# Gate projections of six output tiles as seven block products for a pair of tiles in place of eight

## What is computed

```
z = h @ w_in                    # its last 3 x 1024 columns are the gates g
gates = sigmoid(g)
m = gates[0] * ya + gates[1] * yb + gates[2] * yc
x = layernorm(ALPHA * x + m @ w_out)
```

## Time and profile before

| | us |
|---|---|
| median of 3 runs | 2054.28 |
| the profiled execution, its own time | 2056.70 |
| its span, first to last instruction | 2054.9 |
| mix stage from the branches of tile 0 on, layer 0: 1392 matmuls | 183.51 |
| the same in layer 1 | 183.51 |

### The profile page before, as it was taken

One profiled execution on the slowest core, in us unless ns is written; L12 is line 12 of the kernel. 1 busy time (PEld: TensorE's weight loads), 2 busy tenths in 40 slices (PEclk: granted clock), 3 DMA queues, 4 the chain that ended last, 5 costly groups with the idle time before them and its releaser, 6 DMA issues.

```text
span 2054.9 us, 42901 instructions
## 1 busy us (share of the span) xinstructions
PE 2009.7 (98%) x17322; PEld 1862.5 (91%) x17322; DVE 1195.7 (58%) x2096; ACT 781.6 (38%) x1496; POOL 244.7 (12%) x262
## 2 busy tenths in 40 slices
PE   8999999999999999999999999999999999999997
PEld 8976667999999999999999766689999999999997
DVE  4864445333577652667868544453335876446676
ACT  5443345222344332334454433342222443223344
POOL 0025661000000000000002356600000000000000
PEclk9999999999999999999999999999999999999999
DMA  7349996222412222225345599942223122312261
GB/s 271 124 156 356 369 356 236 72 82 84 134 45 72 82 99 69 82 82 193 128 147 183 200 362 369 364 146 82 84 88 111 46 88 85 103 62 82 85 213 61
DMA packets 84522, 310.90 MB, mean 151 GB/s; under 512 B 10096, under 2 KB 15088, under 8 KB 84016
## 3 DMA queue, kind: packets, MB, share of 16 engines
q1 hardware_dynamic: 42480, 154.83, 23.2%
q0 software_dynamic: 37152, 144.98, 19.1%
q10 hardware_dynamic: 4768, 9.37, 1.4%
HBM read 300.84 MB, written 7.26 MB: 150 GB/s over the span
## 4 chain that ended last, share of the span: by engine, by line
PE 88%; DVE 4%; DMA 3%; ACT 2%; issue 1%; POOL 1%; DVEq 1%; PEldq 0%; ACTq 0%; PEld 0%; POOLq 0%; SPq 0%
PE PS L1021 70%; PE PS L1310 5%; PE PS L1280 5%; DMA m_RAW<-in_cache_wide,m_IDXS 2%; PE PS L1301 1%; DVE m_WL L1452 1%; PE PS L1291 1%; POOL m_RAW L497 1%; DMA m_WS<-in_w_units 1%; ACT m_WH L513 1%; PE PS L1333 1%; PE PS L1349 1%; PE PS L1340 1%; PE PS L1327 0%; ACT m_LS L536 0%
## 5 line engine op out<-in xcount | busy, mean ns | idle before, releaser
L1021 PE MATMUL PS<-m_XS,m_WH 128*128 128x288 f32 x5120 | 908.7, 295 | 10.9 <-DVE m_XS L1452 10.3
L1021 PEld LDWEIGHTS PS<-m_XS,m_WH 128*128 128x128 f32 x5120 | 759.7, 189 | 14.9 <-DVE m_WL L1452 8.1
L1021 PE MATMUL PS<-m_XS,m_WL 128*128 128x288 f32 x2560 | 580.6, 296 | 0.0
L1452 DVE TENSOR_TENSOR m_WL<-m_WS,m_WH 128x1024 fp32r<-128x1024 f32 (+1 forms) x256 | 332.6, 1301 | 200.4 <-ACT m_WH L513 186.6
L1021 PEld LDWEIGHTS PS<-m_XS,m_WL 128*128 128x128 f32 x2560 | 421.1, 188 | 0.0
L513 ACT ACTIVATE m_WH<-m_WS 128x1024 fp32r<-128x1024 f32 (+1 forms) x256 | 285.7, 1118 | 311.9 <-PE PS L1021 281.3
L497 POOL DMA_INDIRECT m_RAW<-in_cache_wide,m_IDXS x256 | 243.4, 951 | 328.0 <-PE PS L1310 99.9
L1021 PE MATMUL PS<-m_HH,m_WH 128*128 128x288 f32 x704 | 202.7, 295 | 2.2 <-DVE m_X L1517 1.9
L1021 PE MATMUL PS<-m_HL,m_WH 128*128 128x288 f32 x704 | 201.7, 295 | 0.0
L1021 PE MATMUL PS<-m_HH,m_WL 128*128 128x288 f32 x704 | 179.2, 295 | 0.0
L1021 PEld LDWEIGHTS PS<-m_HH,m_WH 128*128 128x128 f32 x704 | 132.3, 188 | 3.3 <-DVE m_WL L1452 2.3
(11 more groups left out here) (276 smaller groups left out, 2732.1 us busy)
## 6 DMA issues: line engine op xcount, KB each, us to landing
m_WS<-in_w_units SPq DMA_DIRECT2D x204, 512.0 KB
m_WS<-in_w_units SPq DMA_DIRECT2D x48, 704.0 KB
m_RAW<-in_cache_wide,m_IDXS POOLq DMA_INDIRECT x256
m_X<-in_x_t SPq DMA_DIRECT2D x6, 576.0 KB, 5.9
m_WS<-in_w_units SPq DMA_DIRECT2D x4, 576.0 KB
x_save<-m_X POOLq DMA_DIRECT2D x2, 1152.0 KB, 5.4
m_X<-x_save SPq DMA_DIRECT2D x4, 576.0 KB, 7.4
out_y<-m_X SPq DMA_DIRECT2D x8, 288.0 KB, 2.2
```

The lines of the kernel that those rows point to most:

```text
L1021: mm = pe.matmul(out(half), w(part, k), x(k)[:, half_of(half)], start=(k == 0 and part == 0 and x is xh), stop=(k == last and part == 1))
L1452: return dve.tensor_tensor(out, x, hi.bitcast(F32), ALU.subtract)
```

## The change

Tiles 0 and 1 of m stay as they are, but for work put between their steps. Tiles 2 to 7 are made as three pairs; in each pair the three gates and the branches are nine groups (three for each pair, `GROUPS = 9` in a layer). For one gate of two tiles the weights form a 2x2 block matrix (k 0-3 and 4-7 by first and second tile), and x another (k 0-3 and 4-7 by first and second 288 columns); seven products of blocks replace eight. A product is 4 steps k of one half: 12 matmuls.

- **x side, once a layer:** four VectorE operations of 128x1152 make the differences of x blocks (in place in `X`, one into `D3`), four ScalarE copies and four VectorE subtractions of 128x1152 split them (`difference_hi`, `difference_lo`). Two pairs of these stand between tiles 0 and 1, two within tile 1. As `X` is overwritten, its rows are fetched again at the end of the stage (`rows_back`: four transfers of 128x4x288).
- **weight side, per group:** two raw units land in `GATE_RAW`; VectorE makes four sums of 128x512 in place (`slot_lo`: three at product 0, one at product 4); the seven block weights are split as 128x512 slots and the two branch weights as 128x256 or 128x512 slots, nine slots a group (`PLACES`), in a ring of four. `slot_hi(s)` waits for the product of slot s-4.
- **results, per group:** products go to banks 4, 5, 6, 7, 4, 6, 7; ScalarE copies the first one to `SIG`; seven VectorE additions of 128x288 from PSUM build both gates; two sigmoids in place; then per tile the multiplication by the branch product, and from the second group of a pair on the addition into the mix; in the third group the split into `MH`, `ML`.
- Some 20 semaphores are merged into fewer with other counts, and units of `w_out` land in other raw tiles.

```diff
-                units(l, U_MIX + 2, W_MIX + 2, 30, D)
-                sp.wait_ge(S["ol_mm"], (l + 1) * 2)
+                units(l, U_MIX + 2, W_MIX + 2, 6, D)
+                sp.wait_ge(S["ol_mm"], (l + 1) * 3)
...
+                sp.wait_ge(S["gw_lo"], l * NSLOT + (GROUPS - 1) * PLACES + PRODUCTS)
+                past(sp)
+                fetch(l, U_OUT + 1, W_OUT + 1, D)
+                fetch(l, U_OUT + 3, W_OUT + 3, D)
+                sp.wait_ge(S["gp_done"], (l + 1) * GROUPS * PRODUCTS - 1)
+                past(sp)
+                rows_back(0)
+                sp.wait_ge(S["gw_lo"], (l + 1) * NSLOT)
+                past(sp)
+                fetch(l, U_OUT + 2, W_OUT + 2, D)
+                rows_back(1)
...
 # ScalarE
                 mix_tile(0, first=True)
-                with act.Fori(1, DT) as i:
-                    mix_tile(i)
+                act.wait_ge(S["t_made"], l + 1)
+                difference_hi(XR[:, first_k, early], X[:, first_k, late])
+                difference_hi(D2H[:, :, :], X[:, second_k, late])
+                mix_tile(1)
+                slot_hi(3)
+                for s in range(NSLOT):
+                    if s + 4 < NSLOT:
+                        slot_hi(s + 4)
+                    slot_after(s)
...
 # TensorE
+                def gate_product(n, r):
+                    s = n * PLACES + r
+                    if r == 4:
+                        pe.wait_ge(S["gp_copied"], l * GROUPS + n + 1)
+                    else:
+                        pe.wait_ge(S["g_sums"], (l * GROUPS + n) * 7 + max(0, r - 4))
...
+                    pe.wait_ge(S["gw_lo"], l * NSLOT + s + 1)
...
+                    for k in range(KH):
+                        mm = three(out, w(0, k), w(1, k), xh[:, k, :], xl[:, k, :], k == 0, k == KH - 1)
...
-                with pe.Fori(1, DT) as i:
-                    mix_tile(i)
+                mix_tile(1)
+                for n in range(GROUPS):
+                    for r in range(PRODUCTS):
+                        gate_product(n, r)
+                    for e in range(2):
+                        branch_product(n, e)
 # VectorE
+                def slot_lo(s):
+                    dve.wait_ge(S["gw_hi"], l * NSLOT + s + 1)
+                    lo(slot_part(1, s), slot_source(s), slot_part(0, s)).then_inc(S["gw_lo"], 1)
+                    n, r = s // PLACES, s % PLACES
+                    first, second = raw_tiles(n)
+                    if r == 0:
+                        gates_landed(dve, l, n)
+                        dve.tensor_tensor(SUM_A, in_two(second[:, lower]), in_two(second[:, upper]), ALU.add)\
+                            .then_inc(S["gw_sum"], 1)
...
+                def slot_after(s):
...
+                    if 2 <= r < PRODUCTS:
+                        slot_done(dve, l, s)
+                    if r == 2:
+                        dve.wait_ge(S["gp_copied"], l * GROUPS + n + 1)
+                        add(late_a, early_a, 6)
+                        dve.drain()
...
+                    if r >= PRODUCTS:
...
+                        dve.wait_ge(S["g_sig"], (l * GROUPS + n + 1) * 2)
+                        slot_done(dve, l, s)
+                        dve.tensor_tensor(h2(MT[:, :] if g else out), pair(e), h2(SIG[:, e, :]), ALU.mult)\
+                            .then_inc(S[f"mm_free{e}"], 1)
+                        dve.drain()
+                        if g:
+                            ins = dve.tensor_tensor(out, out, MT[:, :], ALU.add)
+                            if g == 2:
+                                ins.then_inc(S["m_sum"], 1)
+                                dve.wait_ge(S["m_hi"], l * DT + i + 1)
+                                lo(ML[:, i, :], out, MH[:, i, :]).then_inc(S["m_lo"], 1)
+                            else:
+                                dve.drain()
...
                 mix_tile(0, first=True)
-                with dve.Fori(1, DT) as i:
-                    mix_tile(i)
+                dve.tensor_tensor(D3[:, :, :], X[:, second_k, late], X[:, first_k, late], ALU.subtract)
+                dve.tensor_tensor(X[:, first_k, late], X[:, first_k, late], X[:, first_k, early], ALU.subtract)
+                dve.drain()
+                dve.tensor_tensor(X[:, second_k, late], X[:, second_k, late], X[:, first_k, late], ALU.subtract)
+                dve.drain()
+                dve.tensor_tensor(X[:, second_k, early], X[:, second_k, early], X[:, second_k, late], ALU.subtract)
+                dve.drain().then_inc(S["t_made"], 1)
+                difference_lo(1, XR[:, first_k, late], X[:, first_k, late], XR[:, first_k, early])
+                difference_lo(2, XR[:, second_k, late], X[:, second_k, late], D2H[:, :, :])
+                mix_tile(1)
+                slot_lo(3)
+                for s in range(NSLOT):
+                    slot_after(s)
+                    if s + 4 < NSLOT:
+                        slot_lo(s + 4)
+                    if s == NSLOT - 6:
+                        weight_lo(l * NU + U_OUT)
+                    if s == NSLOT - 2:
+                        weight_lo(l * NU + U_OUT + 1)
```

More of the change, by code:

```diff
@@ new lines, in branches @@
+                def branches(n):
+                    c0, width = BRANCH_AT[n % 3]
+                    for e in range(2):
+                        if n:
+                            sp.wait_ge(S["gw_lo"], l * NSLOT + (n - 1) * PLACES + PRODUCTS + e + 1)
+                            past(sp)
+                        unit = W_MIX + 4 * (2 * (FIRST_PAIR + n // 3) + e) + 3
+                        sp.dma_start(BR[e][:, 0:width], w_units[l * NW + unit, :, c0:c0 + width])\
+                            .then_inc(S[f"bw_landed{e}"], 16)
@@ new lines, in rows_back @@
+                def rows_back(half):
+                    for k in (first_k, second_k):
+                        sp.dma_start(X[:, k, half_of(half)], (x_save if l else x_t)[:, k, half_of(half)])\
+                            .then_inc(S["x_in_b" if half else "x_back"], 16)
+                gates(0)
+                for n in range(GROUPS):
+                    if n + 1 < GROUPS:
+                        gates(n + 1)
+                    else:
+                        fetch(l, U_OUT, W_OUT, D)
+                    branches(n)
@@ L453, in _ @@
+                for u in range(4, DT):
                     fetch(l, U_OUT + u, W_OUT + u, D)
@@ L913, in mix_tile @@
                     act.wait_ge(S["mm_done1"], CREDIT["mm_done1"] + l * NM + M_MIX + 3 * i + 3)
-                    weight_hi_in_loop(1, LANDING[l * NU + U_MIX + 5] + 2 * i)
+                    if first:
+                        weight_hi_in_loop(1, LANDING[l * NU + U_MIX + 5] + 2 * i)
+                    else:
+                        slot_hi(2)
                     act.wait_ge(S["m_sum"], l * DT + i + 1)
@@ L1515, in onto_rows @@
                     h = half_of(half)
+                    if back:
+                        dve.wait_ge(S["x_in_b" if half else "x_back"], 32 * (l + 1 + half))
                     dve.wait_ge(S[f"mm_done{par}"], CREDIT[f"mm_done{par}"] + l * NM + m0 + u // 2 + 1)
@@ L1986, in mix_tile @@
                         .then_inc(S["mm_free1"], 1)
-                    weight_lo_in_loop(u + 4, 0)
+                    if first:
+                        weight_lo_in_loop(u + 4, 0)
+                    else:
+                        difference_lo(3, D3L[:, :, :], D3[:, :, :], XL[:, first_k, late])
+                        difference_lo(4, XR[:, second_k, early], X[:, second_k, early], XH[:, first_k, late])
+                        slot_lo(0)
+                        slot_lo(1)
                     dve.wait_ge(S["mm_done0"], CREDIT["mm_done0"] + m + 3)
```

302 lines of the change are left out of this document (231 added, 71 removed).

## The result

The changed kernel took 2063.34 us (median of 6 runs, 2060.39 to 2066.45) against 2054.12 for the kernel before: 1.0045 times as long, 95% interval 1.0033 to 1.0057, so slower by 9 us. The forecast was 2052.3, with a range up to 2060: the time lies above that range, on the slower side. The profiled execution took 2066.45 with a span of 2064.7, against 2056.70 and 2054.9.

What follows compares the result with a forecast made beforehand. TensorE, busy 98% of the span, was taken as the bound. Of 14.2 us a layer saved, waits give back 13.2, leaving 1.0 a layer, 2.0 in all: median 2052.3 us, range 2045 to 2060.

Steps and rivals of the forecast that it cites:

- What is removed: Mix stage: a gate of two tiles takes 84 matmuls instead of 96, saving 28.5 us, 14.2 a layer.
- the walk: Step-by-step timing of VectorE and ScalarE work against TensorE at four places: 13.2 us a layer given back.
- The four places where TensorE waits: Before tile 1's third gate, entering the first pair, from pair to pair, into w_out: 13.6 us a layer.
- gate: Before tile 1's third gate: TensorE waits for VectorE's weight subtraction, delayed by x differences, 3.3 us with the restart.
- first pair: Entering the first pair: TensorE waits 0.7 us, then 2.2 us before slot 2, for VectorE's steps.
- pair changes: From each pair to the next, twice a layer: waits of 0.9 and 2.0 us for the next group's slots.
- last branch product: Into w_out, from the last group's first branch product: multiplications, split and weight subtraction make TensorE wait 1.0 us.
- VectorE's load: Per pair of tiles, 44.7 us of VectorE against 45.9 of TensorE; above 90% busy from tile 2 to 7.
- Rival (b): VectorE becomes the bound because its steps can't overlap: 3.4 us more a layer, 2059 us; chance 0.15.
- Rival (a): Slots run further ahead, so pair-change waits vanish: 11.7 us less, 2041 us; chance 0.19, including a good part of it.
- Costed at nothing: Transfers, SyncE's queue, merged semaphores, ScalarE's load and the other order of raw tiles: all taken as hidden beside TensorE.
- Rival (c): TensorE's clock halves after new waits: 2 us a layer lost, 2056; at every wait, over 2070; chance 0.08.

Runs made afterwards that it cites:

- Experiment 1: Changed kernel plus unused matmuls filling TensorE's waits before tile 1's third gate and the first products of each pair: 2055.74 us, 1.0006 times the kernel before.
- experiment 3: Changed kernel with the splits of the first two x differences put behind tile 1's third weight split: 2053.08 us, 0.9996 times the kernel before.
- experiment 4: Changed kernel with 24 unused matmuls before tile 1's third gate alone, other waits left bare: 2065.03 us, 1.0045 times the kernel before.
- experiment 7: Changed kernel with m splits, x-difference splits and last weight subtraction moved: 2041.02 us; with 4 and 15 unused matmuls at the first pair's waits, 2038.37.

## Why the prediction was wrong

- **What is removed**, 14.2 us a layer: right. Experiment 1 runs the same products at full clock through the whole stage and matches the walk.
- **The four places where TensorE waits**: right in place and nearly in size. With the 0.24 that each costs beside its idle time: gate 2.8 (said 3.3), first pair 0.8 and 2.2 (0.7 and 2.2), pair changes 1.1 and 2.1 (0.9 and 2.0), last branch product 1.1 (1.0), bank 0.65 (0.6). Nine waits make 14.0 where the walk summed 13.6; the gate, too long by 0.5, balances part of the others, most of them a little too short. By the prediction's own terms two of them were longer than it wrote: 10.9 against 8.6 is 2.3 and not 2.2, and 3.8 against 1.6 is 2.2 and not 2.0. The layer without half clock was forecast at 182.9 and comes out at 183.0 and 183.4.
- **VectorE's load**: 83% from tile 2 to 7 where above 90% was said, by adding overlapping durations and by taking a pair at 45.9 us. Rival (b), VectorE as the bound, did not occur: in dense traffic too the steps of 0.69 us start 0.60 apart, as in rows 5. The Trainium skill ("VectorE: DVE Perf Modes", section "The DRAIN you can't avoid") has the next operation wait until the pipeline is empty, and adds that one that is not held starts earlier; in this trace the start stands 0.09 before the recorded end.
- **Rival (a)**, pair changes that don't reach TensorE: did not occur; it took moving the splits of m to bring it about.
- **Costed at nothing**: transfers, queues and the load of ScalarE. In the stage nothing of them ended a wait.
- **The step that failed** is the clock. The sum took the granted clock of the mix stage before as given while adding nine waits a layer. Rival (c) named the mechanism and its price rightly: 2 us a time (4 us at half clock), measured 1.7 (3.4 us). But it had a chance of 0.08, and the text looked at the 3.3 us wait alone as the likely place. The argument for so small a chance was no row: rows 12 show that the kernel before has no wait above 1.2 us between 60 and 2040 us, so its mix stages said nothing of what a wait of 2 us does. Rows 11 show the clock at half with TensorE idle, but the same trace, 10 us earlier, has it at half with TensorE at work, behind two waits of 1.1 us close together. The prediction did not look there (timeline of PE, then windows):

```profile
2037.48 0.75 PE L1059 MATMUL PS<-m_XS,m_CST 128*128 128x288 f32 x2 [1.10 <-DVE m_XS L1521]
2039.34 3.17 PE L1072 MATMUL PS<-m_LS,m_CST 128*128 128x288 f32 x7 [1.11 <-ACT m_LS L536]
...
2040.00:2042.00 2.00, 2.00 (x6) 1.43 (x5) 1.28 (x4) 1.98 (x6) 0.00 (x0) 0.50 0.00 0
```

This pair of waits stands near the end of all ten profiled executions of this document, and a stretch stands behind it in seven of them. So that waits can have this price could have been read before the change. The four waits a layer of 1.9 us and more should have been priced from both sides, nothing and 1.7 each: 0 to 14 us for the kernel. In the profiled execution the clock fell at six of the eight, 10.2 us. The Trainium skill ("TensorE: Matmul & The Clock Gate", section "Why this matters for your kernels") warns that idle gaps between bursts of matmuls bring half clock, and the trace agrees in kind. The gaps it names are longer than any wait of the changed kernel, though: here 1.87 to 2.56 us were enough, and the measurement decides.
- **The range** ended at 2060 because it left out the worst of (c). The value with a fall at every place, over 2070, stood in the text; it was too high because the short waits had no stretch behind them and the long ones not each time.

What stays open: why the same wait is followed by half clock in one execution or layer and not in the next (1 of 6 in experiment 3, 5 of 6 in experiment 4, at the same places), and why waits up to 2.9 us in the kernel before are followed by it less often than 1.9 in the changed one. The place of a wait in time seems to matter beside its length. In layer 0 of the changed kernel the stretches at the pairs start at 407.70, 458.90 and 510.10, 51.20 apart both times, though the waits ahead of them end 1.30, 0.15 and 0.58 us earlier; in layer 1 of experiment 4 they start at 1424.08, 1475.28 and 1526.48, again 51.20 apart. No run moved one wait in time with its length kept, so this is not shown. Waits between 1.0 and 1.8 us did not occur in these stages; outside them, single ones of 1.0 to 1.7 us, three or more in every kernel, had no stretch behind them, and of five of 2.06 to 2.17 us near 46 and 1048 us three had.

## What to carry to other kernels

When a change takes work off a saturated TensorE and gives it waits in return, the waits have a second price: a stretch of half clock behind those near 2 us, 1.7 us each here. Add it to the sum for every such wait, as a term from nothing to its full size. Then look in the order of the engine that is waited for: steps that nobody on the chain reads soon (here the split of m, the splits of the x differences, a later unit's weights) can go behind those that TensorE waits for; three such moves, with no arithmetic added or taken away, turned 0.45% slower into 0.65% faster. Where a wait can't be moved, matmuls of unused result through it kept the clock in experiments 1 and 7; filling one wait alone (experiment 4) brought nothing that the median shows. And look for the fall in the busy part behind a wait, by windows of 2 us: the list of waits doesn't have it.

## What was not expected of the hardware

- Half clock begins between 0.3 us before and 1.6 us after TensorE has resumed: at the first pair change with the first matmuls (restart at 458.75, stretch from 458.90), at the gate of layer 0 after 1.2 us of dense matmuls (386.02, 387.22). So it is no slow start of the engine: it can fall on matmuls in full flow.
- Waits as short as 1.85 us are followed by it in many cases (25 of the 40 from 1.85 us on), and one of 2.90 us was not.
- Additional work made the kernel faster: 87 useless matmuls a layer in place of idle time, 7.6 us less.
